# Front attention: which operand of the values product stands still, and where the probabilities are scaled

## The chip, the cores and the metric

The program runs on one core of one Trainium2 chip. Its engines are named as the profile names them: PE is TensorE's matrix multiply and PEld its weight loads, DVE is VectorE, ACT is ScalarE, POOL is GpSimd, SP is SyncE, which issues the DMAs. The metric is the device time of one execution in microseconds (us); a lower time is better.

## The reference, cut to what matters

Two transformer-like blocks run one after the other on 256 tokens of width 2048. The first block has two layers, and each begins with a wide projection, a convolution branch and a banded attention. Only the attention is touched, once in each of the two layers. Its core, for a block `b` of 128 queries, is

```python
s = jnp.einsum('bqkgd,bskd->bkgqs', qb, kb, preferred_element_type=jnp.float32) * scale + bias_band
s = jnp.where(valid, s, NEG)
m = jnp.maximum(jnp.max(s, axis=-1), sink_f)
e = jnp.exp(s - m[..., None])
denom = jnp.sum(e, axis=-1) + jnp.exp(sink_f - m)
pr = (e / denom[..., None]).astype(vb.dtype)
return jnp.einsum('bkgqs,bskd->bqkgd', pr, vb)
...
yb = _window_attention(q, k, v, bias_band, sink[i]) * jax.nn.silu(b_z)
h = h + jnp.concatenate([ya, yb], axis=-1) @ w_out[i]
```

There are 16 query heads of 64 channels and 4 key-value heads. Everything is float32.

## The kernel before, in words

The activations are held transposed, with channels on partitions and the 256 tokens along the free axis. A weight matrix is cut into units of 128 x 2048 float32 values. For each unit SP loads it into one of four ring slots, ACT writes its rounded high part `whi` (line 229), and POOL or DVE subtracts to get the low part `low` (lines 241 and 234). PE then runs 16 pairs of matmuls, 512 columns of the high part (line 259, the last one line 262) and 256 columns of the low part (line 260). A unit is the beat of the whole kernel.

`phase_front` handles the first projection of a layer. Its 44 units are numbered `m` from 0 to 43, and a table `SLOTS` says what each yields (convolution values and gates, queries `q`, keys, values, and gates `bz` and `az`). Each engine's program is a loop over `m`, and small steps are hung on chosen values of `m`, so the order on every engine is fixed by the code:

- DVE evicts each unit (`evict`, lines 694 to 705), and in units 2 to 35 runs a quarter of a 31-tap convolution on it (`conv`, lines 723 to 727, about eight instructions).
- The 16 heads are done as 8 pairs `h`. A pair takes four units, called its period here, and each step has its place in it. I call the places by the remainder `x` that the code uses. On PE: `scores(h)` behind unit 9+4h, `transposes(h)` behind unit 12+4h, `values(h)` behind unit 13+4h, `out_turned(h)` behind unit 15+4h.
- On DVE: `biased(h)` in unit 10+4h (scores times a factor plus bias, and the row maximum), `normed(h)` and `mixed(h)` in units 14+4h and 16+4h, `low_part(h)` in unit 17+4h. On ACT: `exps(h)` in unit 11+4h, `probs(h)` in unit 13+4h (it copies the transposed probabilities from PSUM to SBUF), `high(h)` in unit 17+4h.

The tile `sm` (128 queries x 4 combinations of head and query block x 257) holds the scores and then the exponentials; its last column is the sink's. `probsT` holds the transposed probabilities, `v_tok` the values with tokens on partitions, `st` small per-row figures (maximum, sum, reciprocal), and `o_norm` the scaled output.

In `values` of the kernel before, a 128 x 128 piece of `probsT` is loaded as the stationary operand and 64 columns of `v_tok` move over it, 8 matmuls a pair. Each float32 matmul of this sort shows as two instructions in the trace, a transpose as one. The output has queries on partitions. `normed` multiplies it by the reciprocal of the softmax sum, `out_turned` transposes it with two instructions, and `mixed` multiplies by the gate.

Behind pair 6 and pair 7 stand three steps of the convolution branch that will matter. `mean()` on PE, inside unit 37, sums the finished convolution over channels (line 921) and waits for its last instruction on DVE (line 727). `variance` on PE (line 899) stands behind units 38 and 39 and waits for squares made by ACT (lines 646 and 649). After unit 43 come eight groups of small matmuls on `p_hl` and then the first unit of the next stage, which waits for a low part made by DVE (line 234).

Of the kernel before, what the change touches and what calls it, by code (L numbers as in the profile page):

```python
# [9 lines left out]
ALU = mybir.AluOpType  # L10
# [3 lines left out]
P = 128  # L14
D = 2048
T = 256
# [129 lines left out]
def program(nc, xT, pT, weights, params, sinks, rel_bias, lora, positions, consts, onehot, band_mask, masks, inv_freq, table, chunk_mats, out):  # L146
    ctx = ExitStack()
    with ctx:
# [308 lines left out]
        for g in range(6):  # L457
# [18 lines left out]
        v_tok = place("v_tok", [P, 2, KV_HEADS * DH], at=arena + 9992)  # L476
        p_hl = place("p_hl", [P, PE_KB, 2 * T], F32R, at=arena + 10504)
        p_in = place("p_in", [P, PE_KB, T], at=arena + 11528)
        o_norm = place("o_norm", [P, 2, P], at=arena + 12040)
        att_probsT = [place(f"probsT{x}", [P, 8, P], at=area + x * KB * 2 * T) for x in range(2)]  # L480
        att_keysT = [place(f"keysT{x}", [P, KV_HEADS, T], at=area + x * KB * 2 * T + 8 * P) for x in range(2)]
        fr_counts = {"flip_in": 16, "p_in": 16, "p_hi": 1, "p_lo": 1, "gate": 24, "gated": 24, "conv": 1,
                     "tok": 1, "tok_read": 1, "turned": 1, "v_read": 1, "k_read": 1,
                     "sink": 8, "scores": 8, "biased": 8, "top": 8, "neg": 8, "exps": 8, "probsT": 8, "probsT_read": 8,
                     "out": 8, "normed": 8, "outT": 8, "mixed": 8, "hi": 8, "lo": 8,
                     "mean": 1, "centred": 1, "y_sq": 2, "var_mm": 2, "var": 1, "dev": 1, "inv": 1, "scaled": 1,
                     "affine": 8, "th": 8, "once": 8, "w": 8, "w_hi": 8, "w_lo": 8,
                     "e_even": 4, "e_odd": 2, "even_read": 3, "odd_read": 4}
# [15 lines left out]
        def phase_front(l, u0, op, nxt, ready=None, summed=None):  # L504
# [53 lines left out]
            def _(act):  # L558
# [31 lines left out]
                def high(h):  # L590
                    if l == 0 and h == 0:
                        act.wait_ge(*table_out(16))
                    act.wait_ge(*fr["mixed"](h + 1))
                    act.activation(nxt[:, CB + h, 0:T], ps[:, 7, 0:T], ACT.Copy).then_inc(fr["hi"].sem, 1)
# [21 lines left out]
                for m in range(46):  # L616
                    if m == 44:
                        even(0).then_inc(fr["even_read"].sem, 1)
                    if m >= 3 * ahead:
                        act_split(act, u0, m)  # L620
                    if m == 0:
                        if l == 0:
                            act_split(act, u0, 2)
                        stat_act(act, stat)
                    if m == 3:
                        act.wait_ge(*fr["p_in"](16))
                        act.activation(p_hl[:, :, 0:T], p_in[:, :, :], ACT.Copy).then_inc(fr["p_hi"].sem, 1)
                    if m == 7:
                        act.wait_ge(*fr["tok"](1))
                        act.activation(tok_s[:, :, :, :], ps[:, 2:4, :], ACT.Copy).then_inc(fr["tok_read"].sem, 1)  # L630
                        act.wait_ge(*fr["tok_read"](1))
                    if m == 8:
                        act.wait_ge(*fr["turned"](1))
                        act.activation(v_tok[:, :, :], ps[:, 4, :], ACT.Copy).then_inc(fr["v_read"].sem, 1)
                        act.activation(keysT[:, :, :], ps[:, 2:4, :], ACT.Copy).then_inc(fr["k_read"].sem, 1)
                        put_sink(0)
                    h, x = (m - 9) // 4, (m - 9) % 4
                    if x == 2 and 0 <= h < PAIRS:
                        exps(h)
                    if x == 0 and 1 <= h <= PAIRS:  # L640
                        probs(h - 1)
                    if x == 0 and 2 <= h <= PAIRS:
                        high(h - 2)
                    if m == 38:
                        act.wait_ge(*fr["centred"](1))
                        act.activation(y_sq[:, :, :], y_ln[:, 0:4, :], ACT.Square).then_inc(fr["y_sq"].sem, 1)
                    if m == 39:
                        act.wait_ge(*fr["var_mm"](1))
                        act.activation(y_sq[:, :, :], y_ln[:, 4:8, :], ACT.Square).then_inc(fr["y_sq"].sem, 1)
                    if m == 45:  # L650
                        high(PAIRS - 1)
                    if 42 <= m:
                        conv_high(2 * (m - 42))
                        conv_high(2 * (m - 42) + 1)
                    if m < 36:
                        act.wait_ge(mm_done.sem, u0 + m + 1)
                        if m >= 2:
                            act.wait_ge(ev_done.sem, u0 + m + 1)
                        act.activation(halves[m % 2][:, 0:T], ps[:, bank_of(m), T:2 * T], ACT.Copy).then_inc(read.sem, 1)
                    if m in GATED:  # L660
                        gate(m)
                    if m == 40:
                        act.wait_ge(*fr["var"](1))
                        act.activation(t2[:, 0:T], t2[:, 0:T], ACT.Sqrt).then_inc(fr["dev"].sem, 1)
                    if m == 44:
                        even(2).then_inc(fr["even_read"].sem, 1)
                    if 41 <= m < 45:
                        affine(2 * (m - 41))
                        affine(2 * (m - 41) + 1)
                    if m == 44:  # L670
                        even(4).then_inc(ev_done.sem, 1)
                    if m == 45:
                        even(6).then_inc(fr["even_read"].sem, 1)
                        act.wait_ge(*fr["odd_read"](3))
                        act.activation(small[:, 5:6], small[:, 5:6], ACT.Copy).then_inc(ev_done.sem, 1)

            @stage.vector
            def _(v):
# [72 lines left out]
                def normed(h):  # L751
                    s = st[:, h % 3, :]
                    v.wait_ge(*fr["exps"](h + 1))
                    link(v.reciprocal(s[:, 24:28], s[:, 12:16]))
                    v.wait_ge(*fr["out"](h + 1))
                    if h:
                        v.wait_ge(*fr["outT"](h))
                    o = ps[:, 4, 0:T].rearrange("p (e q d) -> p e q d", e=2, q=2)
                    dst = o_norm[:, :, :].rearrange("p q (e d) -> p e q d", e=2)
                    v.tensor_tensor(dst, o, spread(s[:, 24:28].rearrange("p (e q) -> p e q", e=2), DH, 3), ALU.mult).then_inc(fr["normed"].sem, 1)  # L760

                def mixed(h):
                    v.wait_ge(*fr["outT"](h + 1))
                    v.wait_ge(*fr["gated"](GATED.index(SLOTS.index(("bz", h))) + 1))
                    if h:
                        v.wait_ge(*fr["lo"](h))
                    v.scalar_tensor_tensor(ps[:, 7, 0:T], ps[:, 4, T:2 * T], 0.5, bz_s[:, h % 3, :], ALU.mult, ALU.mult).then_inc(fr["mixed"].sem, 1)
# [24 lines left out]
                for m in range(44):  # L792
# [3 lines left out]
                    h, x = (m - 10) // 4, (m - 10) % 4  # L796
                    if x == 0 and 0 <= h < PAIRS:
                        biased(h)
                    if x == 0 and 1 <= h <= PAIRS:
                        normed(h - 1)  # L800
                    if x == 2 and 1 <= h <= PAIRS:
                        mixed(h - 1)
                    if x == 3 and 1 <= h <= PAIRS:
                        low_part(h - 1)
                    if m == 6:
                        v.wait_ge(*fr["p_hi"](1))
# [23 lines left out]
                        product(2 * (m - 41) + 1)  # L830
                gated(43)
                odd(1)
                mixed(PAIRS - 1)
                conv_low(4)
                conv_low(5)
                odd(3)
# [22 lines left out]
            def _(pe):  # L859
# [8 lines left out]
                    mm.then_inc(fr["scores"].sem, 1)  # L868

                def transposes(h):  # L870
                    pe.wait_ge(*fr["exps"](h + 1))
                    for x in range(4):
                        for kb in range(2):
                            y = 2 * x + kb
                            mm = pe.transpose(ps[:, 2 + y // 4, (y % 4) * P:(y % 4) * P + P], sm[:, x, kb * P:kb * P + P], ident[:, :])  # L875
                    mm.then_inc(fr["probsT"].sem, 1)

                def values(h):
                    pe.wait_ge(*fr["probsT_read"](h + 1))
                    if h == 0:  # L880
                        pe.wait_ge(*fr["v_read"](1))
                    else:
                        pe.wait_ge(*fr["mixed"](h))
                    for x in range(4):
                        for kb in range(2):
                            mm = pe.matmul(ps[:, 4, x * DH:x * DH + DH], probsT[:, 2 * x + kb, :], v_tok[:, kb, DH * (h // 2):DH * (h // 2) + DH],  # L886
                                           start=kb == 0, stop=kb == 1)
                    mm.then_inc(fr["out"].sem, 1)

                def out_turned(h):  # L890
                    pe.wait_ge(*fr["normed"](h + 1))
                    for qb in range(2):
                        mm = pe.transpose(ps[:, 4, T + qb * P:T + qb * P + P], o_norm[:, qb, :], ident[:, :])
                    mm.then_inc(fr["outT"].sem, 1)

                def variance(x):
                    pe.wait_ge(*fr["y_sq"](x + 1))
# [26 lines left out]
                for m in range(4 * ahead, 44):  # L924
# [27 lines left out]
                        scores(h)  # L952
                    if x == 3 and 0 <= h < PAIRS:
                        transposes(h)
                    if x == 2 and 1 <= h <= PAIRS:
                        out_turned(h - 1)
                    if m in (38, 39):
                        variance(m - 38)
                pe.wait_ge(*fr["p_lo"](1))
# [1527 lines left out]
```

## Time and profile before

| | |
|---|---|
| median of 3 runs | 2235.05 us (2234.09 to 2235.88) |
| profiled execution, first to last instruction (its span) | 2231.8 us |
| what lies around the span, if that execution took the median | about 3.25 us |
| PE busy | 2197.3 us, 98% |
| DVE, ACT, POOL busy | 1695.6, 1071.7, 546.4 us |
| mean share of the DMA engines in a slice of 55.8 us | mostly 0.4 to 0.5 |
| granted PE clock | 0.998 of full speed over the span |

The first stage of layer 0 runs from about 20 to 319 us of the span and that of layer 1 from about 505 to 803 us. The time of the profiled execution outside its span is not given separately, so the sums are made in microseconds of the span and are then taken off the median. An end of a matmul in the trace is modelled; the distance from one start to the next is the better measure of its cost.

### The profile page before, as it was taken

The numbers are of one execution on the slowest core, as the hardware profiler recorded it, in microseconds if no ns is written. First come the engines' busy times: TensorE is split into PE (matmuls) and PEld (weight loads), VectorE is DVE, ScalarE is ACT, GpSimd is POOL, SyncE is SP. The second block draws the span as 40 slices with busy tenths as digits, with TensorE's granted clock in tenths as the row PEclk, the third lists the DMA queues.
The fourth block names the chain that finished last, engine by engine and source line by source line (L and its number), as shares of the span: only waits on it lengthen the run. The fifth ranks groups of instructions, "written<-read, shape, count | busy, mean of one in ns | idle before, by whom it ended". The sixth has DMA issues, their size and how long they took to land.

```text
span 2231.8 us, 38880 instructions
## 1 busy us (share of the span) xinstructions
PE 2197.3 (98%) x14626; PEld 1929.3 (86%) x14626; DVE 1695.6 (76%) x2875; ACT 1071.7 (48%) x1429; POOL 546.4 (24%) x225
## 2 busy tenths in 40 slices
PE   7999999999999999999999999999999999999997
PEld 6888888888888888899999887888888888888886
DVE  7688678885888588788888666788888884447887
ACT  5445464445454464555554644444444443334454
POOL 4676641017767530110001322200000000000001
PEclk9999999999999999999999999999999999999999
DMA  7454445555554445554445300555555555555554
GB/s 254 169 181 169 155 170 179 188 185 197 177 181 165 144 178 187 187 193 166 165 157 194 114 3 21 192 186 188 187 188 188 188 188 188 188 188 189 188 209 168
DMA packets 69320, 384.89 MB, mean 172 GB/s; under 512 B 15120, under 2 KB 23056, under 8 KB 24272
## 3 DMA queue, kind: packets, MB, share of 16 engines
q1 hardware_dynamic: 69200, 383.22, 48.8%
q8 instruction: 84, 1.38, 0.2%
q14 instruction: 36, 0.29, 0.0%
HBM read 380.02 MB, written 3.18 MB: 172 GB/s over the span
## 4 chain that ended last, share of the span: by engine, by line
PE 92%; DVE 4%; ACT 1%; DMA 1%; issue 1%; POOL 0%; SPq 0%; DVEq 0%; POOLq 0%; ACTq 0%
PE ps L259 47%; PE ps L260 25%; PE ps L262 3%; PE ps L247 3%; PE ps L249 2%; PE ps L248 2%; PE ps L886 1%; DVE low L234 1%; PE ps L867 1%; DMA raw<-weights_dram 1%; PE ps L875 1%; PE ps L1882 1%; PE ps L1934 0%; PE ps L1926 0%; ACT whi L229 0%
## 5 line engine op out<-in xcount | busy, mean ns | idle before, releaser
L259 PE MATMUL ps<-opA,whi 128*128 128x512 f32 x2460 | 871.9, 395 | 0.3 <-DVE low L234 0.3
L260 PE MATMUL ps<-opA,low 128*128 128x256 f32 x2624 | 706.7, 279 | 0.2 <-DVE opA L1004 0.2
L229 ACT ACTIVATE whi<-raw 128x2048 fp32r<-128x2048 f32 x346 | 660.2, 1909 | 77.4 <-DMA raw<-weights_dram 76.2
L234 DVE TENSOR_TENSOR low<-raw,whi 128x2048 fp32r<-128x2048 f32 x252 | 583.3, 2315 | 67.8 <-ACT whi L229 52.2
L259 PEld LDWEIGHTS ps<-opA,whi 128*128 128x128 f32 x2460 | 461.0, 187 | 106.2 <-issue 2.8
L241 POOL TENSOR_TENSOR low<-raw,whi 128x2048 fp32r<-128x2048 f32 x95 | 436.6, 4606 | 433.6 <-ACT whi L229 407.2
L259 PE MATMUL ps<-opB,whi 128*128 128x512 f32 x1380 | 494.5, 398 | 14.9 <-DVE opB L418 12.1
L260 PEld LDWEIGHTS ps<-opA,low 128*128 128x128 f32 x2624 | 492.0, 188 | 14.3 <-DVE opA L1004 0.5
L260 PE MATMUL ps<-opB,low 128*128 128x256 f32 x1472 | 397.3, 280 | 0.0
L259 PEld LDWEIGHTS ps<-opB,whi 128*128 128x128 f32 x1380 | 259.7, 188 | 78.1 <-DVE low L412 10.5
L268 ACT ACTIVATE crossed<-ps 128x256 f32<-128x256 f32 x168 | 64.6, 384 | 490.6 <-PE ps L262 490.4
L260 PEld LDWEIGHTS ps<-opB,low 128*128 128x128 f32 x1472 | 277.2, 188 | 7.3
L725 DVE SCALAR_TENSOR_TENSOR ps<-a_in,par,ps 128x256 f32<-128x256 f32 x464 | 226.8, 489 | 14.6
L259 PE MATMUL ps<-act_hl,whi 128*128 128x512 f32 x672 | 237.3, 394 | 0.2
L1147 POOL MEMSET ssq<- 128x256 f32 (+1 forms) x4 | 1.5, 367 | 805.0 <-DVE t L996 677.2
L260 PE MATMUL ps<-act_hl,low 128*128 128x256 f32 x704 | 191.5, 279 | 0.0
L247 PE MATMUL ps<-opB,whi 128*128 128x256 f32 x560 | 161.2, 288 | 0.2 <-DVE ps L1456 0.2
L249 PE MATMUL ps<-opB,low 128*128 128x256 f32 x560 | 158.1, 282 | 0.0
L248 PE MATMUL ps<-opB,whi 128*128 128x256 f32 x560 | 157.7, 282 | 0.0
L259 PEld LDWEIGHTS ps<-act_hl,whi 128*128 128x128 f32 x672 | 125.9, 187 | 30.8 <-issue 2.1
L260 PEld LDWEIGHTS ps<-act_hl,low 128*128 128x128 f32 x704 | 132.0, 187 | 2.6
L1151 POOL TENSOR_TENSOR ssq<-ssq,sq 128x256 f32<-128x256 f32 (+1 forms) x63 | 61.8, 982 | 248.1 <-ACT sq L1064 183.2
(399 smaller groups left out, 2660.9 us busy)
## 6 DMA issues: line engine op xcount, KB each, us to landing
raw<-weights_dram SPq DMA_DIRECT2D x350, 1024.0 KB, 4.8
bias_t<-table_dram SPq DMA_DIRECT2D x16, 384.0 KB, 6.0
hT<-xT_dram SPq DMA_DIRECT2D x4, 512.0 KB, 9.0
out_dram<-hT SPq DMA_DIRECT2D x3, 512.0 KB, 2.8
lora_g<-lora_dram SPq DMA_DIRECT2D x1, 1024.0 KB, 5.1
p_in<-pT_dram SPq DMA_DIRECT2D x2, 256.0 KB, 5.2
lora_wa<-lora_dram SPq DMA_DIRECT2D x1, 512.0 KB, 5.5
chunk_mats_dram<-compact SPq DMA_DIRECT2D x4, 128.0 KB, 3.9
```

Source lines behind the costliest of these rows:

```text
L229: act.activation(whi[:, v % RING, :], raw[:, v % RING, :], ACT.Copy).then_inc(hi_done.sem, 1)
L234: v_.tensor_tensor(wlo(v % RING, 0, width), raw[:, v % RING, 0:width], whi[:, v % RING, 0:width].bitcast(F32), ALU.subtract).then_inc(lo_d ...
L241: pool.tensor_tensor(wlo(v % RING), raw[:, v % RING, :], whi[:, v % RING, :].bitcast(F32), ALU.subtract).then_inc(lo_done.sem, 1)
L247: pe.matmul(dst, whi[:, s, w0:w0 + P], op[:, k, 0:T], start=start, stop=False)
L248: pe.matmul(dst, whi[:, s, w0:w0 + P], op[:, k, T:2 * T], start=False, stop=False)
L249: return pe.matmul(dst, wlo(s, w0, w0 + P), op[:, k, 0:T], start=False, stop=stop)
L259: pe.matmul(*cross, start=start, stop=False)
L260: mm = pe.matmul(ps[:, b, 0:T], wlo(s, w0, w0 + P), op[:, k, 0:T], start=False, stop=False)
L262: mm = pe.matmul(*cross, start=False, stop=True)
L268: act.activation(crossed[:, b, :], ps[:, b if bank is None else bank, T:2 * T], ACT.Copy).then_inc(read.sem, 1)
L725: link(v.scalar_tensor_tensor(y, taps, w, y, ALU.mult, ALU.add))
L1151: pool.tensor_tensor(total, total, part, ALU.add).then_inc(summed.sem, 1)
```

## The change

`values` now loads 64 columns of `v_tok` as the stationary operand and moves 256 columns of `probsT` over them. It takes 4 matmuls a pair, and the two heads of the pair are written to PSUM partitions 0 to 63 and 64 to 127. The output comes out with channels on partitions, so `out_turned` and `o_norm` are gone. The scale can then no longer be applied to the output rows; `normed` applies it to the exponentials in `sm`, in place, before they are transposed. `mixed`, `low_part` and `high` move to earlier places.

```diff
-                    if x == 0 and 2 <= h <= PAIRS:
-                        high(h - 2)
+                    if x == 2 and 1 <= h <= PAIRS:
+                        high(h - 1)
...
-                    if m == 45:
-                        high(PAIRS - 1)
...
                     v.wait_ge(*fr["exps"](h + 1))
                     link(v.reciprocal(s[:, 24:28], s[:, 12:16]))
+                    v.tensor_tensor(sm[:, :, 0:T], sm[:, :, 0:T], spread(s[:, 24:28], T, 2), ALU.mult).then_inc(fr["normed"].sem, 1)
+
+                def mixed(h):
                     v.wait_ge(*fr["out"](h + 1))
-                    if h:
-                        v.wait_ge(*fr["outT"](h))
-                    o = ps[:, 4, 0:T].rearrange("p (e q d) -> p e q d", e=2, q=2)
-                    dst = o_norm[:, :, :].rearrange("p q (e d) -> p e q d", e=2)
-                    v.tensor_tensor(dst, o, spread(s[:, 24:28].rearrange("p (e q) -> p e q", e=2), DH, 3), ALU.mult).then_inc(fr["normed"].sem, 1)
-
-                def mixed(h):
-                    v.wait_ge(*fr["outT"](h + 1))
...
+                    if x == 1 and 0 <= h < PAIRS:
+                        normed(h)
                     if x == 0 and 1 <= h <= PAIRS:
-                        normed(h - 1)
+                        mixed(h - 1)
                     if x == 2 and 1 <= h <= PAIRS:
-                        mixed(h - 1)
-                    if x == 3 and 1 <= h <= PAIRS:
                         low_part(h - 1)
...
                 odd(1)
-                mixed(PAIRS - 1)
...
                 def transposes(h):
-                    pe.wait_ge(*fr["exps"](h + 1))
+                    pe.wait_ge(*fr["normed"](h + 1))
...
-                    for x in range(4):
-                        for kb in range(2):
-                            mm = pe.matmul(ps[:, 4, x * DH:x * DH + DH], probsT[:, 2 * x + kb, :], v_tok[:, kb, DH * (h // 2):DH * (h // 2) + DH],
-                                           start=kb == 0, stop=kb == 1)
+                    for kb in range(2):
+                        for e in range(2):
+                            mm = pe.matmul(ps[DH * e:DH * e + DH, 4, T:2 * T], v_tok[:, kb, DH * (h // 2):DH * (h // 2) + DH],
+                                           probsT[:, 4 * e + kb:4 * e + kb + 3:2, :], start=kb == 0, stop=kb == 1)
                     mm.then_inc(fr["out"].sem, 1)
-
-                def out_turned(h):
-                    pe.wait_ge(*fr["normed"](h + 1))
-                    for qb in range(2):
-                        mm = pe.transpose(ps[:, 4, T + qb * P:T + qb * P + P], o_norm[:, qb, :], ident[:, :])
-                    mm.then_inc(fr["outT"].sem, 1)
...
-                    if x == 2 and 1 <= h <= PAIRS:
-                        out_turned(h - 1)
```

On DVE, the stretch from the eviction of unit 14 to that of unit 15 stood so before (`fr_exps`, `fr_out` and so on are the semaphores waited for; `t_63` and `t_64` are scratch tiles):

```order
L694 TENSOR_TENSOR ps<-ps,t_63 128x256 [waits ev_done,cross_read,dve_step]
L701 SCALAR_TENSOR_TENSOR t_61<-ps,rs 128x256 [waits dve_step]
L713 SCALAR_TENSOR_TENSOR bz_s<-ps,bz_s 128x256 [waits fr_gate]
L745 SCALAR_TENSOR_TENSOR sm<-ps,bias_t 128x2x256 [waits fr_sink,fr_probsT,bias_in1,fr_scores]
L749 TENSOR_REDUCE st<-sm 128x4 [waits fr_biased]
L754 RECIPROCAL st<-st 128x4 [waits fr_exps]
L760 TENSOR_TENSOR o_norm<-ps,st 128x2x2x64 [waits fr_outT,fr_out,dve_step]
L725 SCALAR_TENSOR_TENSOR ps<-a_in,par,ps 128x256 [waits dve_step] x7
L694 TENSOR_TENSOR ps<-ps,t_64 128x256 [waits ev_done,cross_read,dve_step]
L705 TENSOR_TENSOR t_62<-ps,rs 128x256 [waits dve_step]
```

and stands so now:

```order
L742 SCALAR_TENSOR_TENSOR sm<-ps,bias_t 128x2x256 [waits fr_sink,fr_probsT,bias_in1,fr_scores]
L746 TENSOR_REDUCE st<-sm 128x4 [waits fr_biased]
L759 SCALAR_TENSOR_TENSOR ps<-ps,bz_s 128x256 [waits fr_lo,fr_gated,fr_out]
L722 SCALAR_TENSOR_TENSOR ps<-a_in,par,ps 128x256 [waits dve_step] x7
L691 TENSOR_TENSOR ps<-ps,t_64 128x256 [waits ev_done,cross_read,dve_step]
L702 TENSOR_TENSOR t_62<-ps,rs 128x256 [waits dve_step]
L751 RECIPROCAL st<-st 128x4 [waits fr_exps]
L752 TENSOR_TENSOR sm<-sm,st 128x4x256 [waits dve_step]
```

The gate product (`mixed`, L767 before, L759 now) has taken the place of the reciprocal and scale. These stand one unit later, behind the next eviction, and the scale works on 4 x 256 values a row in place of 256.

On PE, the same pair's steps before and now, behind unit 12, 13 and 15 (rows with - are of before, rows with + of now):

```order
-L875 MATMUL ps<-ident,sm 128x128 x8
+L866 MATMUL ps<-ident,sm 128x128 x8
...
-L886 MATMUL ps<-v_tok,probsT_94 128x64 x8
-L867 MATMUL ps<-keysT_96,q_s 128x256 x4
+L877 MATMUL ps<-probsT_93,v_tok 64x256 x4
+L858 MATMUL ps<-keysT_95,q_s 128x256 x4
...
-L893 MATMUL ps<-ident,o_norm 128x128 x2
```

Nothing changes its place on PE; eight matmuls have become four of other operands, and two transposes are gone.

## Rows read from the trace of the kernel before

**Rows 1.** The page: busy time of each engine, and the chain's share by engine.

```profile
PE 2197.3 (98%) x14626; PEld 1929.3 (86%) x14626; DVE 1695.6 (76%) x2875; ACT 1071.7 (48%) x1429; POOL 546.4 (24%) x225
PE 92%; DVE 4%; ACT 1%; DMA 1%; issue 1%; POOL 0%; SPq 0%; DVEq 0%; POOLq 0%; ACTq 0%
```

**Rows 2.** Busy time by stretch: length, PE, PEld, DVE, ACT, POOL, clock, DMA.

```profile
157.00:183.00 26.00, 26.00 (x160) 22.93 (x161) 22.14 (x48) 12.62 (x22) 17.83 (x5) 1.00 0.50 169
```

**Rows 3.** Timeline of PE in two periods of layer 0: start us, us.

```profile
115.06 0.38 PE L893 MATMUL ps<-ident,o_norm 128*128 128x128 f32 x2
...
115.52 0.28 PE L260 MATMUL ps<-opB,low 128*128 128x256 f32 x1
115.63 0.40 PE L259 MATMUL ps<-opB,whi 128*128 128x512 f32 x1
115.87 0.28 PE L260 MATMUL ps<-opB,low 128*128 128x256 f32 x1
...
173.96 1.04 PE L875 MATMUL ps<-ident,sm 128*128 128x128 f32 x8
180.44 1.89 PE L886 MATMUL ps<-v_tok,probsT 128*128 128x64 f32 x16
182.27 1.13 PE L867 MATMUL ps<-keysT,q_s 64*128 64x256 f32 x8
```

**Rows 4.** The chain of waits, merged pieces: start us, us, what.

```profile
63.14 1.90 PE ps L946 x32
...
129.26 1.06 PE ps L867 x8
...
272.45 1.73 PE ps L899 x8
```

**Rows 5.** Timeline of DVE, period of pair 3, with idle time before and its releaser.

```profile
163.18 0.43 DVE L694 TENSOR_TENSOR ps<-ps,t 128x256 f32<-128x256 f32 x1 [2.61 <-ACT t L659]
...
166.77 0.17 DVE L754 RECIPROCAL st<-st 128x4 f32<-128x4 f32 x1
166.98 0.42 DVE L760 TENSOR_TENSOR o_norm<-ps,st 128x256 f32<-128x256 f32 x1
167.32 4.16 DVE L725 SCALAR_TENSOR_TENSOR ps<-a_in,par,ps 128x256 f32<-128x256 f32 x8
171.51 0.43 DVE L694 TENSOR_TENSOR ps<-ps,t 128x256 f32<-128x256 f32 x1
...
172.32 3.10 DVE L725 SCALAR_TENSOR_TENSOR ps<-a_in,par,ps 128x256 f32<-128x256 f32 x6
```

**Rows 6.** Line 425, a DVE product of two SBUF operands: ns min/median/max.

```profile
L425 DVE TENSOR_TENSOR sqs<-sqs x3: 1220/1225/1227, 22.2 to 24.7; 128x1024 f32<-128x1024 f32 x3
```

**Rows 7.** Timeline of POOL around pair 3, then POOL and DVE after the front.

```profile
174.74 9.14 POOL L241 TENSOR_TENSOR low<-raw,whi 128x2048 fp32r<-128x2048 f32 x2 [5.15 <-ACT whi L229]
...
331.62 0.74 POOL L1140 TENSOR_TENSOR ssq<-ssq,e_sq 128x256 f32<-128x256 f32 x1 [2.99 <-ACT e_sq L1069]
...
326.29 0.42 DVE L1000 TENSOR_TENSOR hT<-hT,t 128x256 f32 x1
331.74 0.90 DVE L1000 TENSOR_TENSOR hT<-hT,t 128x256 f32 x1
```

**Rows 8.** Timeline around units 35 to 39: convolution's end, mean, squares, variance.

```profile
255.04 0.48 DVE L727 SCALAR_TENSOR_TENSOR y_ln<-a_in,par,ps 128x256 f32<-128x256 f32 x1
255.58 3.72 PE L921 MATMUL ps<-y_ln,ones 128*128 128x256 f32 x16
278.69 1.04 ACT L649 ACTIVATE y_sq<-y_ln 128x1024 f32<-128x1024 f32 x1
279.85 1.93 PE L899 MATMUL ps<-y_sq,ones 128*128 128x256 f32 x8
```

**Rows 9.** Timeline of the front's last units and the next stage's first matmul.

```profile
307.21 0.70 DVE L272 TENSOR_REDUCE ps<-ps 128x256 f32<-128x512 f32 x1 [0.42 <-PE ps L262]
319.21 0.51 PE L259 MATMUL ps<-opA,whi 128*128 128x512 f32 x1 [0.33 <-DVE low L234]
```

More of the change, by code:

```diff
@@ L478, in program @@
         p_in = place("p_in", [P, PE_KB, T], at=arena + 11528)
-        o_norm = place("o_norm", [P, 2, P], at=arena + 12040)
         att_probsT = [place(f"probsT{x}", [P, 8, P], at=area + x * KB * 2 * T) for x in range(2)]
@@ L484, in program @@
                      "sink": 8, "scores": 8, "biased": 8, "top": 8, "neg": 8, "exps": 8, "probsT": 8, "probsT_read": 8,
-                     "out": 8, "normed": 8, "outT": 8, "mixed": 8, "hi": 8, "lo": 8,
+                     "out": 8, "normed": 8, "mixed": 8, "hi": 8, "lo": 8,
                      "mean": 1, "centred": 1, "y_sq": 2, "var_mm": 2, "var": 1, "dev": 1, "inv": 1, "scaled": 1,
```

## The prediction

> **What bounds the kernel now.** I read the page first. PE is busy for 98% of the span and makes up 92% of the chain that ended last [rows 1], so a microsecond leaves the kernel only if it leaves PE, and it comes back wherever PE is made to wait. Then I read the busy time by stretch over a period of the front [rows 2]: PE 26.00 of 26.00 us, DVE 22.14, POOL 17.83, ACT 12.62. DVE is the second engine, not far behind, and the change gives it work. So I followed PE and DVE through pair 3 (units 21 to 25) in their timelines [rows 3, 5]. The transposes start at 173.96, the values at 180.44, the scores at 182.27. The period is 26.5 us in all middle pairs, and in each of them DVE idles 2.61 us before the eviction at 163.18, where it waits for PE's unit by way of ACT [rows 5]. DVE is re-anchored to PE there once a period.
>
> **The values product.** Before, it takes 182.27 - 180.44 = 1.83 us for 16 instructions of 64 columns, or 0.114 each [rows 3]. After, it takes 8 instructions of 256 columns. What does one cost? Line 899 has 256 columns over a 128 x 128 operand, 8 instructions in 1.73 us, 0.216 each [rows 4]. If the new ones ran one behind the other like these, the step would take 8 x 0.216 = 1.73 us and save 0.10. But line 946 is the nearer row: its stationary operand is 64 columns wide too, and its output alternates between PSUM partitions 0 to 63 and 64 to 127 as here. It does 32 instructions of 128 columns in 1.90 us, 0.059 each [rows 4], where half of line 899's 0.216 would be 0.108. So two instructions of different halves run side by side. By this row the new step takes 8 x 2 x 0.059 = 0.95 us. The scores, 256 columns paired in another way, by halves of the rows, take 1.06 us for 8 [rows 4]. I take 1.02, between the two and nearer to the scores because their column count is the same. The saving is 0.81 a pair; the bounds are 0.10 (no pairing) and 0.91 (8 instructions at the old 0.114).
>
> The Trainium skill ("TensorEngine Tiling (Array Packing)", Column Tiling and Key Properties) says that a stationary operand of up to 64 columns can run as two independent column tiles, up to twice as fast, but that a change of tiling mode drains the engine. Line 946 agrees with the first. The second speaks against the change, since there would be one more change of mode, into the values; no row shows it apart, and the numbers above do not use it.
>
> **The output transposes.** From 115.06 to 115.52 PE does two transposes and one 512-column matmul; without transposes that matmul takes 115.87 - 115.63 = 0.24 [rows 3]. So `out_turned` costs 0.22 a pair, and it goes.
>
> **The scale on DVE.** Reciprocal and scale took 167.32 - 166.77 = 0.55 us [rows 5]. The reciprocal stays, 0.21 to the next start. The scale now covers 1024 elements a row: 1.22 us for such a product of two SBUF operands [rows 6], about 1.14 of it before the next instruction can start, since the last 0.08 overlaps (0.42 us long but 0.34 apart in rows 5, 166.98 to 167.32). Together 1.35, so DVE has 0.80 more a pair. `mixed` and `low_part` only change places. DVE's idle 2.61 shrinks by 0.80 and by what PE gains, 0.81 + 0.22, to about 0.8 us. It stays positive, so DVE still waits for PE once a period and stays hidden: alone it would need 26.5 - 2.61 + 0.80 = 24.7 us a period, PE needs 25.5. If DVE needed 0.8 us more, that cover would be gone, and each further tenth would cost a tenth a pair.
>
> **The new wait.** The transposes of pair h now wait for the scale, which is queued on DVE behind the eviction of unit 11+4h. Pair 3: the eviction starts at 171.51. With `mixed` (0.33) ahead of it in place of 0.55 it starts at 171.29; it takes 172.32 - 171.51 = 0.81 [rows 5], the reciprocal 0.21, the scale 1.22, so the scale ends at 173.53. PE would start the transposes at 173.96 - 0.22 = 173.74 [rows 3], and it has to fetch its first operand before that. That is a tie. I count no stall, and up to 0.3 us a pair in the range. Queued behind the wait on PE are the transposes and the whole of the next unit, so each tenth late is a tenth lost, 1.6 us over 16 pairs.
>
> Behind the scale on DVE stands a quarter of the convolution, 1.1 us later than before in unit 11+4h. In pairs 0 to 5 nobody needs it soon. In pair 6 it is the convolution's last quarter, and PE's `mean()` waits for its end: 255.04 + 0.48 = 255.52, mean at 255.58 [rows 8]. It had no slack. Now it ends at 255.52 - 0.22 + 1.35 = 256.65, while PE arrives 0.22 earlier. The mean starts at 256.71 in place of 255.36: 1.35 us lost in each layer.
>
> **ACT.** `high(6)` now stands ahead of the second square (line 649), behind the exponentials of pair 7. I take 0.28 us for it, an estimate from the 0.34 between starts of a DVE instruction of this size [rows 5]. The square ended at 278.69 + 1.04 = 279.73, and the variance began at 279.85 [rows 8] behind `out_turned(6)`. Now PE wants it at 279.63 and the square ends at 280.01 with 0.06 for the signal: 0.44 lost in each layer.
>
> **The tail.** The last units are tied to ACT and DVE: PE ends unit 43, DVE evicts at 307.21, and 12 us later the first matmul of the next stage starts at 319.21, after 0.33 us of waiting for a low part [rows 9]. `out_turned(7)` lies in that stretch beside the chain, so its 0.22 brings nothing. The values of pair 7 lie before it and do count, as DVE waits 0.42 for PE at 307.21. The moves of `mixed(7)` and `high(7)` fall into waits there.
>
> **The sum.** A layer gives 8 x 0.81 = 6.48 and 8 x 0.22 = 1.76, less 1.35, 0.44 and 0.22: 6.23 us. Two layers give 12.5 us off the profiled span of 2231.8, or 2219.3. The span is 3.25 us under the median of the runs, which I carry over: 2235.05 - 12.5 = 2222.6. All stages behind a front are bound by PE or follow it, so they shift as a whole. DMAs are not touched; the DMA share is 0.50 in the stretch [rows 2].
>
> **Rivals.**
>
> *No pairing.* If the two column halves do not run side by side when they stream different data (line 946 streams one tile into both), the saving is 0.10 a pair: 0.80 + 1.76 - 2.01 = 0.55 a layer, 1.1 in all, 2233.9. Line 946 speaks against it, 32 times in each layer.
>
> *The scale is late everywhere.* If the tie above falls the wrong way by 0.3 us, PE waits in all 16 pairs: 4.8 us come back, 2227.4. The estimate of 173.53 against 173.74 is for it; DVE's durations, which vary by a few ns, are against more.
>
> *The scale meets POOL; slower.* The scale reads two SBUF operands, the old one read PSUM. At 331.74 DVE's line 1000, also with two SBUF operands, took 0.90 us in place of 0.42, and it ended 0.28 after POOL's instruction (331.62 + 0.74 = 332.36) [rows 7]: it waited until POOL was through. POOL's instructions in the front are 4.6 us long. If the scale begins under one, it waits 2.3 us on average, the transposes with it, and 16 x 2.3 = 37 us give about 2259. Slower begins where the scale is late by 12.5 / 16 = 0.8 us a pair. Against it: POOL idles 5.15 us up to 174.74 [rows 7], that is from 169.59, and the scale would run from 172.3 to 173.5, 2.7 us behind POOL's end. It is safe by order too: the POOL instruction at 174.74 needs ACT's split, which stands behind a gate that waits for the same eviction that the scale follows. The rule behind this row is in the Trainium skill ("SBUF — State Buffer", on the port pair shared by DVE and GpSimd): it calls the pair an exclusive lock, held for a whole instruction, and counts a DVE instruction with two SBUF inputs among those that need it. The trace agrees with its 0.90 us.
>
> **How the numbers follow.** About what a measurement of this kernel can tell from no change is 0.2%, or 4.5 us, so faster means under 2230.6. Chances: the forecast 0.70, its own range 2219 to 2226 (saving 0.65 to 0.91 a pair, stalls off by a microsecond or two); late scale 0.15, 2225 to 2231; no pairing 0.09, 2231 to 2235; POOL or another wait on the slow side 0.06. The range 2218 to 2232 leaves out the slow side, most of the case without pairing, and a little below. Faster: 0.70 + 0.14 and a little, 0.85; same 0.09 + 0.01, less a remainder, 0.09; slower 0.06.
>
> **What would show it.** The values should be 8 instructions in about 1.0 us, with nothing at the place of line 893. DVE should have 16 products `sm<-sm,st` of 1.22 us; one that is much longer is a meeting with POOL. Its idle time before the unit of `biased` should fall to 0.8 us. The transposes should wait for little or nothing; the mean should wait 1.3 us for line 724 (the old 727), the variance 0.4 us for the squares. The forecast is wrong if the 8 instructions take 1.7 us, if DVE's idle time in the period is gone and PE waits for evictions, or if the transposes wait for more than a few tenths.

## The result and the profile after

| | before | after |
|---|---|---|
| median | 2234.91 us (4 runs, 2234.09 to 2235.88) | 2222.90 us (4 runs, 2221.58 to 2224.19) |
| ratio after to before | | 0.9947, 95% interval 0.9934 to 0.9960 |
| span of the profiled execution | 2231.8 us | 2219.8 us |
| front of layer 0, first scores to the next stage's first matmul | 319.21 - 76.38 = 242.83 us | 313.73 - 76.39 = 237.34 us |
| the same in layer 1 | 803.38 - 560.53 = 242.85 us | 792.38 - 555.03 = 237.35 us |

The changed kernel is 12.0 us faster, where 12.5 were forecast. The last two rows are the sharpest measure in this case. The two layers agree within 0.02 us, so an experiment's effect of a tenth can be read there, while whole executions spread over 2 to 3 us. The two fronts give 10.99 us of the 12.0. The remaining 1.0 lies behind the last front (1428.4 us before, 1427.4 after), where nothing was changed; the same stretch takes 1426.9 to 1428.6 us in the traces of the experiments, so this 1.0 lies within the spread and cannot be put down to the change. The profiled execution of after took 2221.58 us, so 1.8 us lie around a span, not the 3.25 that I took. Both profiled executions were faster than their kernel's median, by 1.3 us and, if 1.8 holds for before too, by 1.3 us. One execution of e8_one_half (below) ran at a granted clock of 0.556 and took 3596.53 us; its ratio leaves that run out, the median without it is 2236.72, and all other executions of the experiments were at 0.997 or 0.998.

The page after, to be set against [rows 1]; the third line is the chain by engine:

```profile
span 2219.8 us, 38544 instructions
PE 2182.6 (98%) x14466; PEld 1904.6 (86%) x14466; DVE 1708.4 (77%) x2875; ACT 1070.4 (48%) x1429; POOL 545.2 (25%) x225
PE 70%; POOL 14%; issue 12%; DVE 2%; ACT 1%; DMA 1%; SPq 0%; POOLq 0%; DVEq 0%; ACTq 0%
```

PE has 14.7 us less work in a span 12.0 us shorter, and DVE 12.8 us more. The chain's 14% for POOL must not be read as a new bound. PE waits 0.43 us for POOL ahead of the small products behind unit 43, and from there the chain is followed back along POOL, whose instructions alternate with gaps called "issue". PE was busy nearly all the while (98%).

Busy time in one new period, 25.5 us, in the columns of [rows 2]:

```profile
157.00:182.50 25.50, 25.50 (x153) 21.56 (x152) 23.34 (x49) 12.94 (x23) 18.37 (x4) 1.00 0.53 181
```

PE has no idle time, and DVE has risen from 22.14 of 26.0 to 23.34 of 25.5. The timeline of PE, against [rows 3]:

```profile
151.81 0.40 PE L262 MATMUL ps<-opB,whi 128*128 128x512 f32 x1
152.14 1.08 PE L877 MATMUL ps<-probsT,v_tok 128*64 128x256 f32 x8
153.16 1.14 PE L858 MATMUL ps<-keysT,q_s 64*128 64x256 f32 x8
170.91 0.39 PE L262 MATMUL ps<-opB,whi 128*128 128x512 f32 x1
171.15 1.04 PE L866 MATMUL ps<-ident,sm 128*128 128x128 f32 x8
177.72 1.08 PE L877 MATMUL ps<-probsT,v_tok 128*64 128x256 f32 x8
```

The values take 153.16 - 152.14 = 1.02 us. The transposes start 0.24 us after their unit's last matmul, so they do not wait. But the values start 152.14 - 151.81 = 0.33 us after theirs, 0.09 later than a neighbour would. The period is 177.72 - 152.14 = 25.58 us, where it was 26.5.

DVE in the same period, against [rows 5]:

```profile
160.61 0.43 DVE L691 TENSOR_TENSOR ps<-ps,t 128x256 f32<-128x256 f32 x1 [0.87 <-ACT t L656]
168.72 0.43 DVE L691 TENSOR_TENSOR ps<-ps,t 128x256 f32<-128x256 f32 x1
169.53 0.17 DVE L751 RECIPROCAL st<-st 128x4 f32<-128x4 f32 x1
169.73 1.22 DVE L752 TENSOR_TENSOR sm<-sm,st 128x1024 f32<-128x1024 f32 x1
170.87 3.11 DVE L722 SCALAR_TENSOR_TENSOR ps<-a_in,par,ps 128x256 f32<-128x256 f32 x6
```

DVE's idle time fell from 2.61 to 0.87 us (0.8 forecast), and the scale takes 1.22 us and ends at 170.95, 0.20 before the transposes start. All 16 scales took 1.224 to 1.227 us, so none met POOL, which stands still around them (here from 167.21 to 171.95):

```profile
158.00 9.21 POOL L241 TENSOR_TENSOR low<-raw,whi 128x2048 fp32r<-128x2048 f32 x2 [2.50 <-ACT whi L229]
171.95 9.16 POOL L241 TENSOR_TENSOR low<-raw,whi 128x2048 fp32r<-128x2048 f32 x2 [4.74 <-ACT whi L229]
```

The places where PE does wait, against [rows 8, 9]:

```profile
250.77 0.48 DVE L724 SCALAR_TENSOR_TENSOR y_ln<-a_in,par,ps 128x256 f32<-128x256 f32 x1
251.30 3.72 PE L906 MATMUL ps<-y_ln,ones 128*128 128x256 f32 x16 [1.31 <-DVE y_ln L724]
275.08 2.00 PE L884 MATMUL ps<-y_sq,ones 128*128 128x256 f32 x8 [0.27 <-ACT y_sq L648]
302.12 0.36 PE L247 MATMUL ps<-p_hl,whi 128*128 128x256 f32 x1 [0.43 <-POOL low L241]
```

The mean waits 1.31 us for the convolution that the scale has pushed back, and the variance waits for the squares, as forecast. The third wait, for POOL, was not forecast; it costs nothing that can be seen, as the account below shows.

### The profile page after: what moved, and what is told of

Its sections match the earlier page's. It is cut to its first block, busy times and chain, and to the rows that moved or that the text cites. A ratio compares the mean times of both kernels' runs of the same rounds, so it can differ in the third digit from the quotient of the medians.

```text
span 2219.8 us, 38544 instructions
## 1 busy us (share of the span) xinstructions
PE 2182.6 (98%) x14466; PEld 1904.6 (86%) x14466; DVE 1708.4 (77%) x2875; ACT 1070.4 (48%) x1429; POOL 545.2 (25%) x225
## 4 chain that ended last, share of the span: by engine, by line
PE 70%; POOL 14%; issue 12%; DVE 2%; ACT 1%; DMA 1%; SPq 0%; POOLq 0%; DVEq 0%; ACTq 0%
PE ps L259 33%; PE ps L260 18%; POOL low L241 13%; PE ps L247 4%; PE ps L248 3%; PE ps L249 3%; PE ps L262 2%; DMA raw<-weights_dram 1%; PE ps L1865 1%; PE ps L1917 0%; PE ps L1909 0%; PE ps L1717 0%; PE ps L1854 0%; PE ps L298 0%; PE ps L1926 0%
```

## Experiments

Each is an edit of the changed kernel unless said otherwise. "Front" is the mean of the two layers' stretches as in the table above: 242.84 us before, 237.35 after. Medians are of 5 to 11 runs, beside 9 to 19 runs of before on the same chip.

| run | median | before beside it | ratio, 95% interval | front |
|---|---|---|---|---|
| e1_halves_apart | 2222.28 | 2233.34 | 0.9953 (0.9939 to 0.9966) | 237.35 |
| e2_no_scale | 2220.81 | 2233.34 | 0.9945 (0.9932 to 0.9959) | 236.05 |
| e3_mean_later | 2219.90 | 2233.34 | 0.9938 (0.9925 to 0.9952) | 235.72 |
| e4_both_mended | 2219.37 | 2233.34 | 0.9937 (0.9923 to 0.9950) | 235.48 |
| e5_scale_late | 2228.07 | 2233.89 | 0.9973 (0.9962 to 0.9983) | 239.70 |
| e6_meet_pool | 2222.15 | 2233.89 | 0.9948 (0.9935 to 0.9962) | 237.36 |
| e7_before_not_turned | 2231.51 | 2233.89 | 0.9990 (0.9981 to 0.9999) | 241.68 |
| e8_one_half | 2236.78 | 2233.72 | 1.0014 (1.0004 to 1.0024) | 244.24 |
| e9_full_width | 2234.32 | 2233.72 | 1.0004 (0.9994 to 1.0014) | 243.03 |

**Do the column halves run side by side?** The first try changed the order alone:

```diff
-                    for kb in range(2):
-                        for e in range(2):
+                    for e in range(2):
+                        for kb in range(2):
```

> The changed kernel with the two loops of the values product swapped: both blocks of keys of head 0, then both of head 1, so the instructions of one column half follow each other (4 of the first, then 4 of the second) and do not alternate two by two. Theory (the halves run side by side only when instructions of different halves are neighbours): the step grows from 1.02 us to between 1.3 and 1.7 us, all on PE, 0.3 to 0.7 us in each of 16 pairs, 5 to 11 us in all: 2228 to 2234. Rival (a stationary operand of 64 columns is cheaper by itself, in any order): step and time stay, 2223.

Nothing moved: the step, the period and the front are the same to a hundredth, and the median too. Taken alone this spoke for the rival, that a narrow stationary operand is cheap by itself. Two more kernels settled it, both with the loops as in e1. The first puts both outputs in one half:

```diff
-                            mm = pe.matmul(ps[DH * e:DH * e + DH, 4, T:2 * T], v_tok[:, kb, DH * (h // 2):DH * (h // 2) + DH],
+                            mm = pe.matmul(ps[0:DH, 4, T * e:T * e + T], v_tok[:, kb, DH * (h // 2):DH * (h // 2) + DH],
```

> The changed kernel with the loops as in e1_halves_apart and both heads' outputs written to PSUM partitions 0 to 63, side by side in the free axis, so no instruction uses the other column half (the upper head's result is then not the reference's). Theory now (a stationary operand of 64 columns makes an instruction of 256 float32 columns cost 0.13 us by itself): the step stays 1.02 us and the time 2223. Rival (the halves run side by side, in a wider window than two instructions): nothing is left to pair, 8 x 0.216 = 1.73 us, the period grows by 0.7 us and the time by 11 us, 2234.

and the second uses the full width:

```diff
-                            mm = pe.matmul(ps[DH * e:DH * e + DH, 4, T:2 * T], v_tok[:, kb, DH * (h // 2):DH * (h // 2) + DH],
+                            mm = pe.matmul(ps[:, 4, T * e:T * e + T], v_tok[:, kb, P * (h // 4):P * (h // 4) + P],
```

> As e8, but the stationary operand is 128 columns of the values (two key-value heads) and the output fills all 128 partitions; half of it is of no use, so the result is not the reference's. Both theories: 8 instructions at line 899's 0.216 us, 1.73 us, less the 0.1 us that the first instruction of 64 columns starts late; the period grows by 0.6 us, the time by 10 us, 2232. If it stays at 1.02 us, the gain came from the 256 moving columns and fewer instructions alone, and neither the width nor the halves matter.

PE's timeline of e8, and then of e9:

```profile
154.63 0.40 PE L262 MATMUL ps<-opB,whi 128*128 128x512 f32 x1
154.96 1.94 PE L877 MATMUL ps<-probsT,v_tok 128*64 128x256 f32 x8
156.83 1.13 PE L858 MATMUL ps<-keysT,q_s 64*128 64x256 f32 x8
```

```profile
153.31 0.40 PE L262 MATMUL ps<-opB,whi 128*128 128x512 f32 x1
153.55 1.89 PE L877 MATMUL ps<-probsT,v_tok 128*128 128x256 f32 x8
155.37 1.13 PE L858 MATMUL ps<-keysT,q_s 64*128 64x256 f32 x8
```

With one half in use, the same eight instructions with the same 64-column operands take 156.83 - 154.96 = 1.87 us in place of 1.02, and the front grows by 6.89 us, 0.86 a pair (0.7 was expected). So the theory that e8 was run with is wrong and its rival right: the halves do run side by side, and neighbours in the program are not needed for it. The full width takes 155.37 - 153.55 = 1.82 us. That is the old form's 1.83 [rows 3]: exchanging the operands, with half as many instructions, is worth 0.01 us a pair, and everything that the values product gained is the pairing. The period says the same: 26.30 us in e9, and 26.30 in e7 below, which has the old product and no output transposes either.

e9 is the whole change without the pairing. Its fronts are 243.03 - 242.84 = 0.19 us longer than those of the kernel before, and its time is no different (ratio 1.0004, interval 0.9994 to 1.0014). So of the 5.49 us that a front gained, the pairing is 243.03 - 237.35 = 5.68, and all the rest of the change together is -0.19. The period is 0.71 us longer than the changed kernel's, where 0.6 was expected.

The weight loads of the values product (PEld), first in the changed kernel and then in e9, show one more difference:

```profile
152.14 0.63 PEld L877 LDWEIGHTS ps<-probsT,v_tok 128*64 128x64 f32 x8 [0.25 <-issue]
```

```profile
153.32 1.72 PEld L877 LDWEIGHTS ps<-probsT,v_tok 128*128 128x128 f32 x8
```

At full width the first load starts with the unit's last matmul (153.32 against 153.31) and the product 0.24 us behind that matmul. With 64 columns the load starts only with its own product, 152.14 - 151.81 = 0.33 us behind it. Both kernels wait for the same semaphores there, and ACT's copy of the probabilities had ended 2.8 to 2.9 us before in both, so no wait explains it.

How the chip pairs instructions that stand four places apart is open; the traces show no more than that the eight start two at a time in both orders.

**Is the scale hidden, and where not?** The scale left out:

```diff
-                    link(v.reciprocal(s[:, 24:28], s[:, 12:16]))
-                    v.tensor_tensor(sm[:, :, 0:T], sm[:, :, 0:T], spread(s[:, 24:28], T, 2), ALU.mult).then_inc(fr["normed"].sem, 1)
+                    v.reciprocal(s[:, 24:28], s[:, 12:16]).then_inc(fr["normed"].sem, 1)
...
-                    pe.wait_ge(*fr["normed"](h + 1))
+                    pe.wait_ge(*fr["exps"](h + 1))
```

> The changed kernel without the scale: the product with the reciprocal is left out and the transposes wait for the exponentials only. Theory (the scale is hidden behind PE everywhere but ahead of the mean): the convolution ends 1.14 us earlier in unit 35, PE's wait ahead of the mean falls from 1.3 to about 0.2 us, transposes start no earlier, 2.3 us less in all: 2220.6. Rival A (the transposes wait for the scale a little in each pair): 2 to 5 us more come off, 2216 to 2218. Rival B (DVE has enough slack even there): 2223.

The period stays at 25.59 us, so the scale costs nothing in seven of eight pairs. The front falls by 1.30 us and the wait ahead of the mean is gone:

```profile
249.36 0.40 PE L259 MATMUL ps<-opB,whi 128*128 128x512 f32 x1
249.89 3.72 PE L905 MATMUL ps<-y_ln,ones 128*128 128x256 f32 x16
```

The theory holds, with 2.6 us in place of 2.3; rival A is out. And how near is the scale to being late?

```diff
                     link(v.reciprocal(s[:, 24:28], s[:, 12:16]))
+                    link(v.tensor_tensor(extra_t[:, :], rs[:, :], rs[:, :], ALU.add))
```

> The changed kernel with one more DVE sum of 128 x 256 between the reciprocal and the scale, 0.34 us from start to start. Theory (the scale ends 0.2 us before the transposes start, without more slack): the transposes start 0.15 to 0.35 us late in each of 16 pairs and the mean 0.34 us later in each layer, 3 to 6 us more: 2226 to 2229. Rival (the transposes have more slack than the 0.2 us that starts and ends show): only the mean moves, 0.7 us more, 2223.6.

DVE and PE of this kernel:

```profile
170.47 0.43 DVE L753 TENSOR_TENSOR extra_t<-rs 128x256 f32<-128x256 f32 x1
170.93 1.23 DVE L754 TENSOR_TENSOR sm<-sm,st 128x1024 f32<-128x1024 f32 x1
```

```profile
171.66 0.40 PE L262 MATMUL ps<-opB,whi 128*128 128x512 f32 x1
172.21 1.09 PE L868 MATMUL ps<-ident,sm 128*128 128x128 f32 x8 [0.16 <-DVE sm L754]
```

The added instruction puts the scale 0.46 us back, with the wait for its own end. The transposes start 0.55 us after their unit's last matmul, 0.31 more than in the changed kernel, and the period grows by 0.37 to 25.96 us. The front grows by 2.35 us a layer, 4.7 in all. So the first 0.09 to 0.15 us of the 0.46 were free, and the changed kernel stands that near to the edge. The slack of 0.2 between an end on DVE and a start on PE is not all free, since the operand's load comes first. These are the loads of the transposes in the changed kernel and in e2, where no scale stands ahead of them:

```profile
171.01 0.93 PEld L866 LDWEIGHTS ps<-ident,sm 128*128 128x128 f32 x8
```

```profile
170.80 1.02 PEld L865 LDWEIGHTS ps<-ident,sm 128*128 128x128 f32 x8
```

In e2 the load starts 0.01 us after the start of the unit's last matmul, in the changed kernel 171.01 - 170.91 = 0.10 after it and 0.06 after the scale's end. The load already waits for the scale there; the matmul does not yet.

Not every pair stands at this edge, as the expectation had it. Unit by unit, pairs 1 to 5 lose 0.37 us each, and pair 6 loses 0.45 together with the mean behind it. Pair 0, whose scale used to end 0.52 us ahead of the transposes, loses 0.04, and pair 7, where that was 4.8 us, nothing. That sums to 2.34.

**Can the two waits be mended?**

```diff
-                    pe_unit(pe, u0, m, 0, op, ready=ready if m == 0 else None, wide=True, within=(3, mean) if m == 37 else None)
+                    pe_unit(pe, u0, m, 0, op, ready=ready if m == 0 else None, wide=True, within=(8, mean) if m == 37 else None)
```

> The changed kernel with the mean's matmuls put behind the 8th of the 16 blocks of unit 37 and not behind the 3rd, 1.75 us later. Theory: the 1.3 us wait ahead of the mean is covered by the unit's own matmuls and nothing behind it waits for the mean so soon; 2.6 us less: 2220.3. Rival (the wait only moves to the squares or the variance behind units 37 and 38): 2223.

The front falls by 1.63 us in each layer, 3.3 in all, more than the 2.6 expected. The wait itself was 1.31; the rest I put down to the lost overlap of the first operand's load behind a wait, which no run shows apart. In e4 the second square goes first as well:

```diff
-                    if x == 2 and 1 <= h <= PAIRS:
+                    if m != 39 and x == 2 and 1 <= h <= PAIRS:
                         high(h - 1)
...
                         act.activation(y_sq[:, :, :], y_ln[:, 4:8, :], ACT.Square).then_inc(fr["y_sq"].sem, 1)
+                        high(h - 1)
```

> As e3_mean_later, and in unit 39 ACT makes the second square before the rounding of pair 6 and not after it. Theory: the variance no longer waits, 0.44 us less in each layer on top of the mean's 1.3: 3.5 us less than the changed kernel, 2219.4. Rival (the second square is not what the variance waits for): as e3, 2220.3.

The front falls by another 0.24 us a layer, where I expected 0.44. From the end of unit 39 to that of unit 40 it is 7.61 us, as it was before with the output transposes in it (0.23), so 0.2 us stayed lost: the square ends no earlier than in the kernel before, and PE now asks for it earlier. This version is the best of the case, 2219.37 us beside 2233.34 on its chip, and its fronts are 1.87 us each shorter than the changed kernel's. The difference of the medians of e3 and e4, 0.5 us, is as large as the fronts say, but a comparison of whole runs alone could not tell it.

**What if DVE meets POOL?** A small sum with two SBUF operands in a place where POOL is at work:

```diff
                     if x == 2 and 1 <= h <= PAIRS:
                         low_part(h - 1)
+                    if x == 2 and 1 <= h < PAIRS:
+                        link(v.tensor_tensor(extra_t[:, :], rs[:, :], rs[:, :], ALU.add))
```

> The changed kernel with one more DVE sum of 128 x 256 with two SBUF operands in unit 12+4h behind the low part of the attention output, at a moment when POOL is some 4 us into one of its 4.6 us subtractions and has the next one right behind. Theory (DVE with two SBUF operands waits until POOL's running instruction is through): the sum takes 0.6 to 0.8 us in place of 0.42, DVE's idle time in the period covers it, the time stays within 1 us, 2223. Rival A (POOL's next instruction gets ahead of the waiting one): the sum takes about 5 us, DVE has no idle time left and PE waits some 4 us a pair, 2270 or more. Rival B (no contention here): 0.42 us, 2223.

All 14 instances (min/median/max in ns), the one of pair 2's place in DVE's timeline, and POOL beside it:

```profile
L799 DVE TENSOR_TENSOR extra_t<-rs x14: 411/725/743, 125.0 to 763.3; 128x256 f32<-128x256 f32 x14
```

```profile
176.19 0.73 DVE L799 TENSOR_TENSOR extra_t<-rs 128x256 f32<-128x256 f32 x1
```

```profile
172.01 9.34 POOL L241 TENSOR_TENSOR low<-raw,whi 128x2048 fp32r<-128x2048 f32 x2 [3.95 <-ACT whi L229]
176.59 4.76 POOL L241 TENSOR_TENSOR low<-raw,whi 128x2048 fp32r<-128x2048 f32 x1
```

The last row is the second of POOL's two by itself; in the changed kernel it stood so:

```profile
176.53 4.58 POOL L241 TENSOR_TENSOR low<-raw,whi 128x2048 fp32r<-128x2048 f32 x1
```

POOL's first instruction ends near 172.01 + 4.6 = 176.6, and DVE's, begun at 176.19, ends 0.3 after that, at 176.92. Alone it takes 0.41, as the two instances show that begin when POOL is through. Ten begin some 0.45 us ahead of POOL's end and take 0.72 to 0.74, and the other two, 0.2 ahead of it, take 0.49 and 0.51. All twelve end 0.3 us after POOL's instruction, so DVE waits for the running one. It does not wait for POOL's next: that one's record starts at 176.59, before DVE's ends, and is 0.18 us longer than without the sum. I read this as DVE getting in ahead and POOL waiting, but the records of POOL are rough and no run shows the order by itself. DVE's idle time hid it and the front did not move. The slower rival of the prediction has its mechanism in this program; what it lacks is the meeting.

**What are the output transposes worth?** This is an edit of the kernel before. `mixed` reads the output untransposed, which changes the result but not the work:

```diff
-                    for qb in range(2):
-                        mm = pe.transpose(ps[:, 4, T + qb * P:T + qb * P + P], o_norm[:, qb, :], ident[:, :])
...
-                    v.scalar_tensor_tensor(ps[:, 7, 0:T], ps[:, 4, T:2 * T], 0.5, bz_s[:, h % 3, :], ALU.mult, ALU.mult).then_inc(fr["mixed"].sem, 1)
+                    v.scalar_tensor_tensor(ps[:, 7, 0:T], ps[:, 4, 0:T], 0.5, bz_s[:, h % 3, :], ALU.mult, ALU.mult).then_inc(fr["mixed"].sem, 1)
```

> The kernel before without the two output transposes of a pair: the gate product reads the scaled pair's PSUM tile as it lies, not turned, and waits for the scale. Theory: 0.22 us less in each pair but the last of a layer, which lies in the tail beside the chain through ACT and DVE; 2 x 7 x 0.22 = 3.1 us less than before, 2231.8. Rival A (the tail's share counts too): 3.5 us less. Rival B (PE has slack at that place): no change, 2234.9.

The period falls by 0.23 us, but the front by only 1.16 us a layer, 2.3 in all and not 3.1. That is 5 pairs' worth, not 7. The share of pair 5 lies ahead of the mean, which is tied to DVE, and that of pair 6 ahead of the variance, which is tied to ACT. Of the three shares that bring nothing, I had named only the last in this expectation.

## Why the prediction was right, point by point

From end to end of PE's units in layer 0, before less after:

| stretch | what is in it | gained, us |
|---|---|---|
| first scores to unit 34 | 6 values, 5 output transposes | 5.41 |
| units 35 and 36 | 1 output transpose | 0.24 |
| unit 37 | the wait for the convolution | -1.38 |
| unit 38 | values of pair 6 | 0.72 |
| unit 39 | nothing changed | 0.00 |
| unit 40 | 1 output transpose, the wait for the squares | -0.27 |
| unit 41 | nothing changed | 0.00 |
| unit 42 | values of pair 7 | 0.76 |
| behind unit 43 | 1 output transpose, beside the chain through ACT and DVE | 0.00 |

The rows sum to 5.48 of the 5.49 measured; 6.23 were forecast. One place in the kernel before belongs to this account, where the scores of pair 0 stand right behind a unit:

```profile
76.05 0.40 PE L262 MATMUL ps<-opB,whi 128*128 128x512 f32 x1
76.38 1.14 PE L867 MATMUL ps<-keysT,q_s 64*128 64x256 f32 x8
76.38 0.73 PEld L867 LDWEIGHTS ps<-keysT,q_s 64*128 64x128 f32 x8 [0.26 <-issue]
```

The load starts only with its own matmul, and that one 76.38 - 76.05 = 0.33 us after the unit's last, not 0.24.

- **The values product: the mechanism right, the size off.** The instructions take the 1.02 us that I took, and pairing carries all of it (e8, e9). But the step saved 0.71 to 0.72 us a pair and not 0.81, because the first instruction now starts 0.09 us late. In pair 7 it waits for ACT's copy in both kernels, starts only 0.02 later, and 0.76 is saved. That makes 7 x 0.09 + 0.05 = 0.68 of the 0.74 us that a layer fell short; the squares below are most of the rest. I had set the late start aside as what no row shows, and that was wrong: the scores of pair 0 show it in the trace of the kernel before, as above. There the operand changes from 128 x 128 to 64 x 128, in the values now to 128 x 64, and in e9, where the shape stays, nothing is late. The Trainium skill ("TensorEngine Tiling (Array Packing)", Key Properties) says that changing the tiling mode drains the engine. The late loads of the scores and the values, and the early one of e9, agree with it.
- **The price of the rival without pairing: too kind.** I gave it a saving of 0.10 a pair, 8 x 0.216 = 1.73 us for 1.83. The step took 1.82 at full width (e9) and 1.87 with one half (e8), mainly because the scores behind it start late too: the old 1.83 held that and my 1.73 did not. Going by the fronts of e9 and e8, the rival would have stood 0.4 to 2.8 us above the kernel before, and not 1.1 below.
- **The output transposes: right.** 0.23 a pair (e7) against 0.22. The last brought nothing, as said, and those of pairs 5 and 6 were spent at the two waits, as the sum had it.
- **The scale: right.** 1.22 us, hidden in seven of eight pairs (e2), with DVE's idle time at 0.87.
- **The tie at the transposes: right, and as close as it looked.** No stall at 0.2 us, and a stall in pairs 1 to 6 once the scale is 0.46 us later (e5). The rival of the late scale counted 16 pairs; pairs 0 and 7 of each layer are not at the tie.
- **The mean and the squares: right.** 1.38 lost against 1.35, and 0.27 + 0.24 = 0.51 (the loss in unit 40 and the transposes that brought nothing) against 0.44.
- **The tail: right in sum, incomplete in its cause.** From the end of unit 43 to the next stage it is 12.43 us before and after. Within it, PE now waits 0.43 us for a low part of POOL's that used to be in time. The values of pair 7 bring PE there 0.76 us earlier, and in e8 and e9, where they are as long as before, this wait is absent. PE's wait of 0.33 us at the end is gone, so the tail has hardly any spare time left on PE.
- **What lies around the span: wrong.** It is 1.8 us and not 3.25. It cancelled in the difference.

## What to carry to other kernels

Follow the wait that a step has after the edit, pair by pair, and not only in the average period: the same 1.1 us on DVE was free seven times and cost more than its own length the eighth, and moving the one step that waited for it was worth 3.3 us (e3). When two edits arrive together, price them apart: here the exchange of operands was worth nothing, and the use of both column halves was worth everything. Before pricing a step that changes the operand's shape, look in the trace for another that does: its late start was on view in pair 0. A removed PE step counts only if what follows it is bound by PE.

## What the runs showed of the hardware that I had not expected

- Eight float32 matmuls of 64 stationary and 256 moving columns take 1.02 us when four write PSUM partitions 0 to 63 and four write 64 to 127, whether they stand two by two or four by four in the program. They take 1.87 us when all write one half.
- At full width they take 1.82 us, so a narrow operand that leaves the other half idle is not cheaper than a wide one.
- Where the stationary operand changes its shape in these traces, the first load does not start under the matmul before it. Behind a unit of 128 x 128 the first product starts 0.33 us after the last matmul's start and not 0.24, for 64 x 128 (scores of pair 0) and 128 x 64 (values) alike.
- A DVE instruction with two SBUF operands that begins under a POOL instruction ends 0.3 us after it (12 of 12 in e6). It does not wait for POOL's next, though that stands right behind.
